# Last layer's gated results of three head groups: turned back by VectorE's 32x32 squares and two transfers instead of by TensorE transposes, the fourth group left on TensorE

## The reference

```python
def fox_layer(x, norm_w, w_in, q_norm_w, out_norm_w, w_out, k, v, F):
    h = rmsnorm(x, norm_w)
    proj = h @ w_in
    q = proj[..., :D_MODEL].reshape(B, T, FOX_HEADS, FOX_HDIM)
    gate = proj[..., D_MODEL:]
    q = head_rmsnorm(q, q_norm_w).transpose(0, 2, 1, 3)
    o = forgetting_attention(q, k, v, F)
    o = head_rmsnorm(o.transpose(0, 2, 1, 3), out_norm_w.reshape(FOX_HEADS, FOX_HDIM))
    o = o.reshape(B, T, D_MODEL) * jax.nn.silu(gate.astype(jnp.float32))
    return x + (o.astype(x.dtype) @ w_out)
```

## Time and profile before

| | |
|---|---|
| median of 3 runs | 1828.15 us (1828.1 to 1828.44) |
| profiled execution | 1828.43 us |
| its span, first to last instruction | 1826.6 us |
| mean granted TensorE clock | 1.000 of full speed |
| TensorE busy | 1813.7 us (99%) |
| VectorE busy | 1267.3 us (69%) |
| ScalarE busy | 942.7 us (52%) |

### The profile page before, as it was taken

One profiled execution on the slowest core, in us unless ns is written; L12 is line 12 of the kernel. 1 busy time (PEld: TensorE's weight loads), 2 busy tenths in 40 slices (PEclk: granted clock), 3 DMA queues, 4 the chain that ended last, 5 costly groups with the idle time before them and its releaser, 6 DMA issues.

```text
span 1826.6 us, 24598 instructions
## 1 busy us (share of the span) xinstructions
PE 1813.7 (99%) x8999; PEld 1531.1 (84%) x8999; DVE 1267.3 (69%) x1711; ACT 942.7 (52%) x1310; POOL 38.0 (2%) x116
## 2 busy tenths in 40 slices
PE   8999999999999999999999999999999999999999
PEld 7899998888888888887888888888888888888887
DVE  6676766588556755767887878787767556577764
ACT  4545554455465555636554545555435444565542
POOL 2000000000000004000000000000000000000000
PEclk9999999999999999999999999999999999999999
DMA  8565454668889887575555555544547776555453
GB/s 293 162 177 148 139 175 156 202 179 185 177 153 212 175 179 176 191 238 159 174 175 152 167 173 154 179 154 160 185 138 232 217 217 209 162 160 163 159 166 113
DMA packets 172909, 323.61 MB, mean 177 GB/s; under 512 B 16584, under 2 KB 23136, under 8 KB 172048
## 3 DMA queue, kind: packets, MB, share of 16 engines
q1 hardware_dynamic: 171680, 317.89, 60.6%
q10 hardware_dynamic: 576, 4.19, 0.6%
q0 software_dynamic: 560, 0.26, 0.1%
HBM read 318.11 MB, written 4.19 MB: 176 GB/s over the span
## 4 chain that ended last, share of the span: by engine, by line
PE 98%; DVE 1%; ACT 0%; DMA 0%; issue 0%; DVEq 0%
PE acc L366 28%; PE acc L368 28%; PE acc L367 27%; PE ps L615 2%; PE ps L2760 2%; PE ps L463 1%; PE acc L332 1%; PE acc L333 1%; PE acc L331 1%; PE ps L648 1%; PE acc L350 0%; PE acc L349 0%; PE acc L353 0%; PE acc L355 0%; PE acc L348 0%; PE acc L354 0%
## 5 line engine op out<-in xcount | busy, mean ns | idle before, releaser
L299 DVE TENSOR_TENSOR wlo<-wraw,whi 128x1024 fp32r<-128x1024 f32 x579 | 699.1, 1222 | 337.4 <-ACT whi L284 334.4
L284 ACT ACTIVATE whi<-wraw 128x1024 fp32r<-128x1024 f32 x579 | 599.9, 1052 | 365.8 <-PE acc L368 333.4
L366 PE MATMUL acc<-whi,ta_hi 128*128 128x512 f32 x1664 | 659.7, 396 | 3.6 <-DVE ta_lo L548 2.0
L368 PE MATMUL acc<-whi,ta_lo 128*128 128x512 f32 x1664 | 649.2, 390 | 0.0
L367 PE MATMUL acc<-wlo,ta_hi 128*128 128x512 f32 x1664 | 647.8, 389 | 0.0
L366 PEld LDWEIGHTS acc<-whi,ta_hi 128*128 128x128 f32 x1664 | 312.6, 188 | 68.7 <-DVE ta_lo L548 3.4
L368 PEld LDWEIGHTS acc<-whi,ta_lo 128*128 128x128 f32 x1664 | 312.3, 188 | 66.9
L367 PEld LDWEIGHTS acc<-wlo,ta_hi 128*128 128x128 f32 x1664 | 312.8, 188 | 62.1
L366 PE MATMUL acc<-whi,tb_hi 128*128 128x512 f32 x576 | 228.4, 396 | 0.0
L368 PE MATMUL acc<-whi,tb_lo 128*128 128x512 f32 x576 | 224.9, 390 | 0.0
L367 PE MATMUL acc<-wlo,tb_hi 128*128 128x512 f32 x576 | 224.4, 390 | 0.0
(11 more groups left out here) (325 smaller groups left out, 1644.8 us busy)
## 6 DMA issues: line engine op xcount, KB each, us to landing
wraw<-in_ml_w_in SPq DMA_DIRECT2D x129, 512.0 KB, 5.8
wraw<-in_a_w_in SPq DMA_DIRECT2D x128, 512.0 KB, 3.9
wraw<-in_kv_w SPq DMA_DIRECT2D x64, 512.0 KB, 4.0
wraw<-in_b_w_in SPq DMA_DIRECT2D x64, 512.0 KB, 4.4
wraw<-in_mla_w_in SPq DMA_DIRECT2D x49, 512.0 KB, 4.6
wraw<-in_mla_w_out SPq DMA_DIRECT2D x32, 512.0 KB, 3.8
wraw<-in_ml_w_out SPq DMA_DIRECT2D x32, 512.0 KB, 4.4
wraw<-in_a_w_out SPq DMA_DIRECT2D x32, 512.0 KB, 3.8
```

The costliest lines, as they stand in the source:

```text
L284: nc.scalar.activation(unit_of(whi, n, SPLIT, w), unit_of(wraw, n, RAW, w), ACT.Copy).then_inc(w_high, 1)
L299: nc.vector.tensor_tensor(unit_of(wlo, n, SPLIT, w), unit_of(wraw, n, RAW, w), unit_of(whi, n, SPLIT, w).bitcast(F32), ALU.subtract).then_ ...
L366: nc.tensor.matmul(o, xh, wh, start=first, stop=False)
L368: m = nc.tensor.matmul(o, xl, wh, start=False, stop=end)
```

## The change

For groups 0, 1 and 2 (`by_squares`) TensorE's 8 transposes of `back` are left out. VectorE, right behind the gate's multiplication in `post`, waits for that multiplication and transposes the 32x32 squares of `o3` into `o3_stage` (the memory of the scores `S3` and of a part of `PT3`), two instructions of 128x512. SP copies the stage out to a new tensor `back_squares` (512 KB) behind the load of the second next group's unit 2, and behind the load of its unit 4 waits for that copy and copies it back into `o3` by four transfers of 128 KB. The step `back` of VectorE and ScalarE moves from u = 28 to u = 31, waits for these transfers, and reads `o3` in place of PSUM. TensorE's wait for `lo` ahead of the next group's queries is left out. Group 3, whose `back` lies in `l3_out`, is as it was.

```diff
+        def by_squares(g):
+            return not (isinstance(g, int) and g == 3)
+        def back_at(g):
+            return L3_AT["back"] + (3 if by_squares(g) else 0)
+        BACK_OUT, BACK_IN = 2, 4
+        back_squares = nc.dram_tensor("back_squares", (P, 2 * COLS), F32).ap()
+        o3_flat = o3.rearrange("p b n -> p (b n)")
+        o3_stage = bass.AP(S3.tensor, S3.offset, [list(S3.ap[0]), [1, 2 * COLS]])
...
+            def turn_back(g, p):
+                if p == BACK_OUT:
+                    sp.wait_ge(l3["b_sq"], TB * (g + 1))
+                    sp.dma_start(back_squares, o3_stage).then_inc(l3["b_out"], 16)
+                if p == BACK_IN:
+                    sp.wait_ge(l3["b_out"], 16 * (g + 1))
+                    for j in range(4):
+                        sp.dma_start(o3_flat[32 * j:32 * j + 32, :].rearrange("q (i r) -> q i r", i=4),
+                                     back_squares.rearrange("(i q) (j r) -> j q i r", i=4, j=4)[j]).then_inc(l3["b_in"], 16)
...
-                    with sp.Fori(1, runs) as it:
+                    for p in range(units(tiles)):
+                        load(name, p, 1)
+                        if name == "l3_kv":
+                            turn_keys(0, p)
+                    with sp.Fori(2, runs) as it:
                         for p in range(units(tiles)):
                             load(name, p, it)
                             if name == "l3_kv":
                                 turn_keys(it - 1, p)
+                            else:
+                                turn_back(it - 2, p)
                 elif runs == 1:
                     for p in range(units(tiles)):
                         load(name, p)
+                        if name == "l3_out":
+                            turn_back(2, p)
...
                     nc.vector.tensor_tensor(flat(o3), flat(gw3), flat(o3), ALU.mult).then_inc(l3["og"], 1)
+                    if by_squares(g):
+                        dve.wait_ge(l3["og"], g + 1)
+                        blocks = o3_stage.rearrange("p (j b h c) -> p b j h c", j=4, b=TB, h=4)
+                        for b in range(TB):
+                            nc.vector.transpose(blocks[:, b], square_columns(o3[:, b, :])).then_inc(l3["b_sq"], 1)
...
                         t = tmpT[:, b, :].rearrange("p (k t) -> p k t", t=P)
-                        dve.wait_ge(l3["ogp"], 2 * g + b + 1)
+                        if by_squares(g):
+                            dve.wait_ge(l3["b_in"], 64 * (g + 1))
+                            y = o3_flat.rearrange("p (i b h c) -> p b h i c", i=4, b=TB, h=4)
+                            w = colB[:, group(64, g)].unsqueeze(2).unsqueeze(3).to_broadcast([P, 4, 4, 32])
+                            nc.vector.tensor_tensor(t.rearrange("p k (i c) -> p k i c", i=4), y[:, b], w,
+                                                    ALU.mult).then_inc(l3["tmp"], 1)
+                            continue
+                        dve.wait_ge(l3["ogp"], b + 1)
...
-                if u == L3_AT["back"] + LAG:
+                if u == back_at(g) + LAG:
                     back()
...
-                    if g > 0:
-                        pe.wait_ge(l3["lo"], 2 * g)
...
-                if u == L3_AT["back"]:
+                if u == L3_AT["back"] and not by_squares(g):
                     back()
```

More of the change, by code:

```diff
@@ L937, in build @@
         l3 = sems(3, "r_dg r_row f_row f_e f_ok sq_out kss qss oss ksq kv_ krs kn kt kT qsq qv qrs qn qt qT sc msk mx ex pt ptc pv o "
-                     "ge gs sq v rs on og ogp tmp hi lo")
+                     "ge gs sq v rs on og ogp b_sq b_out b_in tmp hi lo")
         def dst_l3(name, k, b, it):
```

## The result

The changed kernel takes 1849.33 us (median of 4 executions, 1847.18 to 1850.42), before 1828.28 (1828.1 to 1828.44): a ratio of 1.0113, 95% interval 1.01 to 1.0127. It is 1.1% slower. The predicted 1839.5 had the direction and half of the size; the measured time lies above the range. The profiled execution took 1847.18 us, its span is 1845.5, 18.9 us more than before.

What follows compares the result with a forecast made beforehand. TensorE, busy 99%, was taken as the bound. Per group -0.90 + 1.04 + 0.75 - 0.18 + 3.07 = +3.8 us, three groups +11.3, on 1828.15 gives 1839.5 us; range 1830.5 to 1847.

Steps and rivals of the forecast that it cites:

- TensorE's transposes leave: Ahead of unit 42 in group 1, TensorE's eight transposes drop out: -0.90 us a group.
- VectorE's squares: They make `low` of units 42 and 44 (group 1) late; TensorE waits +1.04 and +0.75 us a group.
- The old wait of unit 29 goes: At unit 45 in group 1, `back` no longer stands ahead of `low`, so TensorE's wait goes: -0.18 us.
- The step `back` behind its transfers: At the scores, TensorE waits for `turned`, behind rounding, VectorE's multiplication and the copies in: +3.07 us a group.
- The landing of 4.3 us for the last copy: The last of four copies in lands 4.3 us after its issue, with bounds of 3.2 and 6.3.
- rival 3: The pause at the scores halves TensorE's clock for scores and one unit: 4.5 us more a group, 1853; chance 0.10.

Runs made afterwards that it cites:

- `turned` first: Changed kernel with ScalarE's next `turned` put ahead of its rounding of `back` in unit 16g + 31: 1833.93 us, ratio 1.003.
- either filling: Changed kernel with unread TensorE work ahead of the `qT` wait in groups 1 to 3: 20 transposes, 1845.59 us, or 9 matmuls, 1846.08 us.
- the faster version: Changed kernel with squares at VectorE's u = 28, copies behind SP's loads of units 4 and 6, `back` at u = 34: 1826.92 us, ratio 0.9991.

## Why the prediction was wrong

Point by point, with its own steps:

- **TensorE's transposes leave, -0.90 a group.** Right: removal alone gave 1826.58, against 1826.6 by the same walk. The 390 ns that the Trainium skill ("VectorE: DVE Perf Modes", The three transpose paths) gives for one transpose in bf16 would have promised 3.1 us a group, as an estimate; the trace had 0.79 for eight of them.
- **VectorE's squares, +1.04 and +0.75.** Right. In group 0 TensorE would have been ready for unit 26 at 1602.29 and started at 1603.28, +0.99; for unit 28 at 1608.85, and started at 1609.47, +0.62 and 0.1 for a longer first matmul. Squares alone cost 3.9 us in three groups, as worked out.
- **The old wait of unit 29 goes, -0.18.** Right, the third wait is gone.
- **The step `back` behind its transfers, +3.07.** The mechanism was right in each link: copies, VectorE's multiplication, rounding, `turned`, scores. The term was mis-sized. **The landing of 4.3 us for the last copy is the first step that failed**: it was 5.0, 4.6 and 5.7, 2.4 us more in all, and in group 2 the four issues took 3.19 us in place of 1.8, another 1.4. The pauses were 3.56, 3.18 and 5.41 us, from start to start some 0.17 more each, so 12.7 us in place of 9.2: **+3.5** (TensorE also reached the scores some 0.1 us later than worked out, which shortens each pause). I had seen the load just ahead in the queue and allowed 0.8 us over the median for it. With that load removed from ahead of them the last copies landed in 3.1 to 4.2.
- **The clock, rival 3. Leaving it out of the sum is the second step that failed.** I gave it 0.10 and tied it to the slowest landings. It came true in two of three groups of the profiled execution, in group 0 at a pause of 3.56 us, half a microsecond over the 3.07 that I forecast. Its price there is the scores alone: 3.39 and 3.50 us in place of 1.77, **+3.3**, where I had put 4.5 a group, since I let the unit behind run at half speed too. The clock was back at 1.00 with that unit.

Together 11.3 + 3.5 + 3.3 = 18.1 of the 18.9 us. The remaining 0.8 lies in small pieces: 0.2 more at the waits for `low`; 0.2 more at the scores, counted from start to start (1.87 us in group 1, 3.58 in group 2); 0.1 that was there ahead of the stage; and 0.3 behind the last matmul, which starts 18.64 us later (1841.43 in place of 1822.79). The other executions took up to 3.2 us more than the profiled one at a mean clock of 0.995 to 0.996 in place of 0.997, which fits one more place at half clock and later copies; they have no trace that would show it.

The error was in the range too. The late landing and the falling clock aren't independent: the clock fell only in or just behind pauses of 2.69 us and more, none of the pauses of up to 1.83 us brought it down, and a pause of 3 us was forecast. So the case of both had to stand inside the range, not beyond its end.

Open is why one issue of a copy took 1.3 to 2.7 us in some groups (in the changed kernel, with `turned` first, with either filling, and in the faster version), and never over 0.5 where the copies went behind the load of unit 3.

## What to carry to other kernels

Ask of every step that gets a wait what stands behind it in the same engine's stream: here two instructions of ScalarE in the wrong order were worth 15 us as long as the copies came late (4.9 once they went out one unit earlier), more than TensorE's transposes saved or VectorE's squares cost. Work for an idle engine is free only at a place where the stream it feeds is ahead; measure that lead unit by unit, since a busy share of 69% hid places with no more than 0.5 us of it. Don't price a small transfer by its median where a large one is issued just ahead of it, be it in its own queue (4.5 us in place of 2.9) or in another (4.5).

## What the runs showed of the hardware that I had not expected

- A copy of 128 KB from DRAM landed in 2.6 to 4.2 us, median 2.9, with no load just ahead, and in 4.0 to 5.7 us, median 4.5, with a load of 512 KB issued 0.5 us ahead in the changed kernel (up to 7.4 at the same place of the kernel filled by matmuls); behind two loads up to 7.6. Issued by GpSimd, with SP's load 1.2 us ahead in group 0, it took 4.0 to 6.6, median 4.5.
- The granted clock fell to half in pauses of 3.56, 5.41 and 2.69 us and 0.7 us behind one of 3.94, and held in one of 3.18 us; the time from the end of TensorE's work to the fall was 2.2 to 4.7 us. It came back within the scores or in the unit behind them. A fall cost 1.6 and 1.8 us in the changed kernel, 1.7 in the one filled by matmuls and 3.1 in the one filled by transposes, where the unit behind the scores still ran at half speed up to 1684.8 us (it reached L648 6.78 us after its first matmul, in place of 5.49).
- VectorE's multiplication of SBUF in runs of 32 numbers took 1.29 us for two of 128x512, the same as from PSUM without such runs.
